# Interleaving full-array and tiled matmuls head by head in a gated linear attention output

## The reference, cut to what matters

```
att = jnp.where(causal, jnp.einsum('nbhid,nbhjd->nbhij', q_dec, k_inv), 0.0)
o_intra = jnp.einsum('nbhij,nbhje->nbhie', att, vc)
...
o_inter = jnp.einsum('bhid,bhde->bhie', q_d, state)
state = state * jnp.exp(decay)[..., None] + jnp.einsum('bhjd,bhje->bhde', k_e, v_c)
...
o = (o_intra + o_inter)
```

## Time and profile before

| | us |
|---|---|
| median of 3 runs | 2661.28 |
| lowest and highest | 2656.83, 2661.81 |
| the profiled execution, its own time | 2661.28 |
| its span in the trace | 2659.4 |
| TensorE busy | 2556.1 |
| TensorE weight loads busy | 2065.7 |
| VectorE busy | 1399.2 |
| ScalarE busy | 1023.4 |

### The profile page before, as it was taken

How to read it: one execution, slowest core, us unless ns; L and a number is a source line. 1 busy time by engine, 2 the same in 40 slices (tenths; PEclk the granted TensorE clock), 3 DMA queues, 4 the chain that set the end, 5 groups by cost and what they waited for, 6 DMA issues and landing times.

```text
span 2659.4 us, 46124 instructions
## 1 busy us (share of the span) xinstructions
PE 2556.1 (96%) x19758; PEld 2065.7 (78%) x19758; DVE 1399.2 (53%) x1950; ACT 1023.4 (38%) x1697; POOL 277.2 (10%) x228
## 2 busy tenths in 40 slices
PE   7999999999998899899999999999999998999998
PEld 5755787778987788678888877788888876788887
DVE  4345698545677433566653556553453456552542
ACT  3245666433333322333333346432223356331222
POOL 0210102223331000101111001100000001100001
PEclk8999999988999999999999999999999999999999
DMA  7100321141003233323233221233223211233222
GB/s 265 58 16 20 107 64 33 51 161 51 4 4 128 91 98 95 119 86 96 95 97 96 88 69 48 79 97 101 95 95 96 87 56 56 87 98 100 95 95 72
DMA packets 64715, 222.91 MB, mean 84 GB/s; under 512 B 7168, under 2 KB 7552, under 8 KB 64384
## 3 DMA queue, kind: packets, MB, share of 16 engines
q1 hardware_dynamic: 63936, 218.39, 25.2%
q10 hardware_dynamic: 576, 1.57, 0.2%
HBM read 213.64 MB, written 6.29 MB: 83 GB/s over the span
## 4 chain that ended last, share of the span: by engine, by line
PE 87%; DVE 8%; issue 2%; ACT 2%; DMA 1%; POOL 0%; SPq 0%; POOLq 0%; DVEq 0%; ACTq 0%
PE ps L321 58%; PE ps L2696 6%; PE ps L1715 5%; PE ps L331 3%; PE ps L837 2%; PE ps L812 1%; PE ps L1721 1%; PE ps L1740 1%; PE ps L1757 1%; DVE w_lo L299 1%; DVE o_tok L1607 1%; PE ps L2749 1%; PE ps L828 1%; PE ps L2779 1%; DMA ring<-in_w_mod_first 1%
## 5 line engine op out<-in xcount | busy, mean ns | idle before, releaser
L299 DVE TENSOR_TENSOR w_lo<-ring,w_hi 128x1024 fp32r<-128x1024 f32 (+1 forms) x339 | 420.7, 1241 | 838.3 <-ACT w_hi L291 838.2
L291 ACT CAST w_hi<-ring 128x1024 fp32r<-128x1024 f32 (+1 forms) x339 | 353.8, 1044 | 918.6 <-PE ps L321 833.0
L321 PE MATMUL ps<-u_hi,w_hi 128*128 128x512 f32 x864 | 338.6, 392 | 9.1 <-DVE u_lo L580 9.1
L321 PE MATMUL ps<-u_lo,w_hi 128*128 128x512 f32 x864 | 336.9, 390 | 0.0
L321 PE MATMUL ps<-u_hi,w_lo 128*128 128x512 f32 x864 | 336.8, 390 | 0.0
L321 PE MATMUL ps<-mid_hi,w_hi 128*128 128x512 f32 x688 | 267.6, 389 | 0.0
L321 PE MATMUL ps<-mid_lo,w_hi 128*128 128x512 f32 x688 | 267.6, 389 | 0.0
L321 PE MATMUL ps<-mid_hi,w_lo 128*128 128x512 f32 x688 | 267.6, 389 | 0.0
L321 PEld LDWEIGHTS ps<-u_hi,w_hi 128*128 128x128 f32 x864 | 162.5, 188 | 46.9 <-issue 8.9
L321 PEld LDWEIGHTS ps<-u_lo,w_hi 128*128 128x128 f32 x864 | 162.7, 188 | 33.9 <-issue 0.5
L321 PEld LDWEIGHTS ps<-u_hi,w_lo 128*128 128x128 f32 x864 | 162.6, 188 | 33.6
(11 more groups left out here) (449 smaller groups left out, 4640.0 us busy)
## 6 DMA issues: line engine op xcount, KB each, us to landing
ring<-in_w_up SPq DMA_DIRECT2D x44, 512.0 KB, 3.5
ring<-in_w_in SPq DMA_DIRECT2D x42, 512.0 KB, 3.5
ring<-in_w_merge SPq DMA_DIRECT2D x32, 512.0 KB, 3.4
ring<-in_w_mlp1a SPq DMA_DIRECT2D x32, 512.0 KB, 3.5
ring<-in_w_mlp2a SPq DMA_DIRECT2D x32, 512.0 KB, 3.5
ring<-in_w_mlp1b SPq DMA_DIRECT2D x32, 512.0 KB, 3.5
ring<-in_w_mlp2b SPq DMA_DIRECT2D x32, 512.0 KB, 3.4
ring<-in_w_gdn_in SPq DMA_DIRECT2D x24, 512.0 KB, 3.5
```

What stands on the lines that cost most here:

```text
L291: nc.scalar.copy(w_hi[:, slot, 0:width], ring[:, n % RING, 0:width]).then_inc(*hi_ok.one())
L299: nc.vector.tensor_tensor(w_lo[:, slot, 0:width], ring[:, n % RING, 0:width], as_f32(w_hi[:, slot, 0:width]), ALU.subtract).then_inc(*lo_o ...
L321: mm = nc.tensor.matmul(dst[:, a:b], w[wi][:, k * P:(k + 1) * P], src[xi][:, k0 + k, a:b], start=start and k == wi == xi == 0, stop=stop a ...
```

## The change

The loop over the heads becomes the outer one within a tile of tokens. Each head does its multiplication over the whole array and directly after it its two small ones, for the two chunks. The set of multiplications, their operands and destinations, and the four increments of `p_ok` stay the same.

```diff
                             for t in range(TL):
-                                dst = [ps[:, OUT_BANKS[h], 64 * t:64 * t + 64] for h in range(4)]
                                 for h in range(4):
-                                    nc.tensor.matmul(dst[h], at_[:, t, h, :], gv[:, t, 64 * h:64 * h + 64],
+                                    r, dst = slice(32 * h, 32 * h + 32), ps[:, OUT_BANKS[h], 64 * t:64 * t + 64]
+                                    nc.tensor.matmul(dst, at_[:, t, h, :], gv[:, t, 64 * h:64 * h + 64],
                                                      start=True, stop=False)
-                                for half in range(2):
-                                    c, q = 2 * t + half, slice(64 * half, 64 * half + 64)
-                                    for h in range(4):
-                                        r = slice(32 * h, 32 * h + 32)
-                                        mm = nc.tensor.matmul(dst[h][q, :], gq[r, c * GLA_C:(c + 1) * GLA_C],
-                                                              st[r, c, :], start=False, stop=True)
-                                        if c == NCH - 1:
-                                            mm.then_inc(*p_ok.one())
+                                    for half in range(2):
+                                        c, q = 2 * t + half, slice(64 * half, 64 * half + 64)
+                                        mm = nc.tensor.matmul(dst[q, :], gq[r, c * GLA_C:(c + 1) * GLA_C], st[r, c, :],
+                                                              start=False, stop=True)
+                                    if t == TL - 1:
+                                        mm.then_inc(*p_ok.one())
```

## The result

| | before | after |
|---|---|---|
| median | 2659.47 us (8 runs) | 2678.51 us (8 runs) |
| lowest and highest | 2653.03, 2663.06 | 2671.17, 2696.71 |
| the profiled execution | 2661.28 us | 2682.11 us |

The medians differ by 19.0 us. The ratio over all executions on record, 41 of the changed kernel, is 1.0082, with a 95% interval of 1.0062 to 1.0102: slower, by 16 to 27 us. The forecast was 2684, a ratio of 1.0085. In the table the changed kernel spreads over 25 us from run to run and the one before over 10; but over the 29 executions beside the later experiments the kernel before spread over 21 as well.

What follows compares the result with a forecast made beforehand. The prediction took TensorE, busy 96% of the span, as the bound. It added 9.4 us for the order and 13.2 us for the low clock, 22.6 in all, to 2661.3: 2684 us, range 2669 to 2690.

Steps and rivals of the forecast that it cites:

- TensorE is the bound and nothing hides the stretch: At `gla_out`, TensorE shows no idle time, so a microsecond added there is a microsecond at the end.
- The ordered cost: In `gla_out`, 32 round trips between 128x128 and 32x64 forms in place of 8: 0.626 us per head, +9.4 us.
- rival 2: In `gla_out`, a head's two halves run one after the other: +3.4 to 7 us on top; chance 0.05.
- rival 3: Not slower: in `gla_out`, small passes slip into the wide weights' load time, 2657 or 2661 us; chance 0.08.
- The fall of the clock in both layers: TensorE's clock falls to 1.2 GHz, 4 us into each layer's `gla_out`, for too little streaming; chance 0.62.
- rival 1: The clock holds in both layers' `gla_out`, leaving only the ordered cost, 2670.7 us; chance 0.17.
- The price of the clock: Low clock in the rest of `gla_out` (+4.7 us) and dense products behind (+1.9): 6.6 per layer, +13.2 us.
- the second term: The low clock's cost in `gla_out` and the dense products behind it, +13.2 us for two layers.

Runs made afterwards that it cites:

- the pair of spread-out kernels: Kernel before with `gla_out`'s token tiles put between quarters of HEAD+1's dense product, once in the new order (ratio 1.0052), once in the old (1.0042).
- the half-way order: Against the kernel before: two heads' wide multiplications, then their four small ones, 16 round trips in place of 8; ratio 1.0031.
- no change of form: Changed kernel with each head's two small multiplications made one over the whole array, so the result differs from the reference; ratio 1.0008 to the kernel before.
- diagonal: Kernel before, old order, with each wide multiplication split into two 64x64 products on the array's diagonal tiles, same result; ratio 0.9988.

## Why the prediction held, point by point

- **TensorE is the bound and nothing hides the stretch:** right. `gla_out` grew by 12.88 - 5.24 = 7.6 us in the first layer and the stage by 10.4; the rest, 2.7, is the low clock in the products behind it. In the second layer it grew by 12.80 - 5.24 = 7.6 and the stage by 8.9. Nothing was absorbed.
- **The ordered cost, +9.4:** right. The head takes 0.63 us against a forecast of 0.626, and the pair of spread-out kernels gives 4.65 us per layer, 9.3 in all, with no low clock in it. The way down and back didn't become cheaper after bursts of two.
- **The halves in series (rival 2):** didn't happen; four passes of a head last 0.33 with a way back of the old length. **Not slower (rival 3):** no small pass moved into the shadow of a load.
- **The fall of the clock in both layers:** right, and rival 1 with it wrong. TensorE was never idle there; the rule of rival 1, by which the clock falls behind idle stretches alone, does not describe this case. But the step to it was thinner than it reads. Both falls in the earlier trace rows stood behind stretches that had idle time in them, 2.58 us and 4.00 - 2.67 = 1.33 us, and no row showed a fall without any. That the reason given, too little streaming, is the right one isn't shown: no run separates it from the changes of form.
- **The price of the clock, +13.2:** this term was mis-sized. It measured 19.3 - 9.3 = 10.0 us (5.8 and 4.2). Three of its parts were off. The fall came 5.2 us into `gla_out` (1564.0 against 1558.83), not 4, so 4.7 us of work was left in place of 5.9. The factor was 1.64 (1.03 over 0.63), not the 1.8 of a burst of eight. Split like the period in the prediction, the two wide passes of a head went from 0.156 to 0.27 us, the ways down and back from 0.36 to 0.59 and the small passes from 0.113 to 0.17: no part grew by more than 1.7, and the ways are more than half of a head. (The 1.8 compares the lengths of two rows, and these contain the recorded length of the last pass. From the start of each burst to the start of the next row it is 2.01 against 1.00 us, so it was not the right reading for a burst of eight either.) The late fall and the factor together make + 3.0 us per layer in place of 4.7. The dense products ran low for 5.9 us in the first layer and 2.7 in the second, where I had 4: + 2.7 and + 1.2 at 46%, which with 3.0 each makes 5.7 and 4.2.
- **The sum:** 9.3 + 10.0 = 19.3, against 22.6 forecast. The profiled pair differs by 20.8. The 1.5 us outside the two stages are not accounted for.

What stays open: why the clock falls where it does, and why it needed 5.9 us of dense work in one layer and 2.7 in the other. The split into 9.3 and 10.0 is that of one execution. The other executions have no trace, but each has its mean granted clock, and it bears the second term out. The mean of these was 0.983 over 54 executions of the kernel before; it was 0.978 over 41 of the changed kernel, 0.980 over 6 with the small ones one head later, 0.981 over 12 of the half-way order, and 0.982 or 0.983 where the trace shows no fall in the two stages (new order between dense products, no change of form, no small ones, diagonal). The spread of the changed kernel goes with it: the three executions at 0.984 or 0.985 took 2671 to 2673 us, the three at 0.968 to 0.971 took 2694 to 2697. The first three lie 12 to 13 us above the median before, nearer to the ordered cost alone; whether the clock held in their `gla_out` can't be seen without a trace.

## What to carry to other kernels

Price an order of small matmuls by its changes of form and not by its instruction count. Here each added round trip between the whole array and 32x64 tiles cost 0.39 us, so many of one form belong in one burst. When such a stretch gets longer on TensorE, look also at what the granted clock will do to it and to the dense products behind it: here that doubled the loss, while a busy share of 100% showed nothing. If the scattered work can't be avoided, put dense products between its pieces: in the traced execution they kept the clock up. They can delay what hangs on the result, here the first scores by 1.5 us.

## What the runs showed of the hardware that I had not expected

- A `gla_out` in which TensorE was never idle was granted 0.50 from 3.3 to 5.3 us after its start, in all six cases with added round trips and nothing dense between them, while one filled with whole-array passes of 64 columns kept 1.00 for 7 us.
- Time spent in changes of form grows by less than 2 at the low clock: the ways down and back of a head went from 0.36 to 0.59 us and the whole head from 0.63 to 1.03, when dense 512-column matmuls go from 0.23 to 0.43 apart.
- Two 64x64 tiles on the diagonal take 0.91 us per token tile where the whole array takes 1.335 for the same result. A load of 64 columns is recorded with 0.13 us and one of 128 with 0.19, and the loads follow each other 0.028 us apart in place of 0.111.
